# Which engine asks for the down weights: moving one expert weight in three from SyncE's queue to ScalarE's

## The reference, cut to what matters

```python
def hier_moe(xn, w_gr, b_gr, w_er, b_er, w_gate, w_up, w_down):
    ...
    def expert_block(args):
        tok_b, e = args
        xb = xpad[tok_b]
        h = jax.nn.silu(xb @ w_gate[e]) * (xb @ w_up[e])
        return h @ w_down[e]
    ...
    out = out.reshape(rows, d) * buf_wt[:, None].astype(out.dtype)
    y = jnp.zeros((t + 1, d), out.dtype).at[buf_tok].add(out)[:t]
```

## Time and profile before

| | us |
|---|---|
| median of three runs | 1744.66 |
| lowest and highest | 1743.45, 1745.66 |
| the profiled execution | 1749.66 |
| its span | 1747.6 |
| expert stage in it, about | 170 to 677 |
| one pair of experts at full TensorE clock | 30.5 |

### The profile page before, as it was taken

One profiled execution on the slowest core, in us unless ns is written; L12 is line 12 of the kernel. 1 busy time (PEld: TensorE's weight loads), 2 busy tenths in 40 slices (PEclk: granted clock), 3 DMA queues, 4 the chain that ended last, 5 costly groups with the idle time before them and its releaser, 6 DMA issues.

```text
span 1747.6 us, 24578 instructions
## 1 busy us (share of the span) xinstructions
PE 1628.3 (93%) x9324; PEld 1305.9 (75%) x9324; DVE 1249.0 (71%) x1537; ACT 780.7 (45%) x1021; POOL 393.5 (23%) x184
## 2 busy tenths in 40 slices
PE   7995899999999997999988999999999999999997
PEld 7855555555555554988678999999999978888886
DVE  5244888878888886765315996566777788888886
ACT  4413777767777774456033334666666400000000
POOL 6601211111111110000234889422222100000000
PEclk9996899999999998999999999999999999999999
DMA  8407799999999988533312444444444555555553
GB/s 315 154 1 302 304 421 409 415 373 392 421 408 411 413 345 275 193 121 121 145 49 92 175 169 166 150 148 151 141 152 150 187 193 186 194 194 194 192 192 120
DMA packets 45902, 398.87 MB, mean 228 GB/s; under 512 B 10120, under 2 KB 12424, under 8 KB 13576
## 3 DMA queue, kind: packets, MB, share of 16 engines
q1 hardware_dynamic: 45832, 397.89, 59.4%
HBM read 395.77 MB, written 3.01 MB: 228 GB/s over the span
## 4 chain that ended last, share of the span: by engine, by line
PE 38%; POOL 6%; issue 4%; DMA 1%; DVE 1%; ACT 0%; DVEq 0%; POOLq 0%; SPq 0%
PE bank L1834 19%; PE bank L1771 9%; POOL rest L1010 6%; PE bank L1775 5%; PE bank L1805 3%; PE bank L763 1%; DMA raw<-in_v 1%; POOL ring_rest L742 0%; DVE lead L2305 0%; DVE h L2404 0%; ACT half_lead L736 0%; DVE hid_lo L2379 0%; DVE h L2407 0%; DVE xhat L656 0%; DVEq L188 0%
## 5 line engine op out<-in xcount | busy, mean ns | idle before, releaser
L2067 DVE TENSOR_TENSOR ring_rest<-ring,w_lead 128x2048 fp32r<-128x2048 f32 x128 | 293.4, 2343 | 37.7 <-ACT w_lead L1144 37.7
L1144 ACT ACTIVATE w_lead<-ring 128x2048 fp32r<-128x2048 f32 x128 | 239.4, 1905 | 22.1 <-DVE ring_rest L2067 21.7
L647 ACT ACTIVATE xhat<-h 128x1024 f32<-128x1024 f32 x6 | 6.3, 1057 | 432.9 <-DVE h L2404 351.8
L1571 PE MATMUL bank<-ring_rest,x_two 128*128 128x512 f32 x512 | 140.9, 408 | 31.7 <-DVE ring_rest L2067 31.7
L1289 ACT ACTIVATE lead<-raw 128x2048 fp32r<-128x2048 f32 x64 | 122.4, 1913 | 88.7 <-PE bank L1775 88.7
L1834 PE MATMUL bank<-lead,hid_hi 128*128 128x512 f32 x512 | 157.9, 390 | 2.7 <-DVE hid_lo L2379 2.6
L1834 PE MATMUL bank<-lead,hid_lo 128*128 128x512 f32 x512 | 157.7, 389 | 0.0
L1834 PE MATMUL bank<-rest,hid_hi 128*128 128x512 f32 x512 | 157.6, 389 | 0.0
L1571 PE MATMUL bank<-w_lead,x_two 128*128 128x512 f32 x512 | 145.9, 423 | 11.8 <-POOL x_two L993 6.6
L1775 PE MATMUL bank<-nT_hi,rest 128*128 128x256 f32 x1024 | 144.7, 284 | 9.7 <-POOL rest L1010 9.7
L742 POOL TENSOR_TENSOR ring_rest<-ring,half_lead 128x2048 fp32r<-128x2048 f32 x20 | 92.4, 4627 | 264.2 <-ACT half_lead L736 255.0
(11 more groups left out here) (331 smaller groups left out, 2831.0 us busy)
## 6 DMA issues: line engine op xcount, KB each, us to landing
ring<-in_w_gate SPq DMA_DIRECT2D x32, 2048.0 KB, 9.4
ring<-in_w_up SPq DMA_DIRECT2D x32, 2048.0 KB, 9.6
ring<-in_w_down SPq DMA_DIRECT2D x32, 2048.0 KB, 10.4
raw<-in_u SPq DMA_DIRECT2D x64, 1024.0 KB, 4.8
raw<-in_v SPq DMA_DIRECT2D x64, 1024.0 KB, 4.8
ring<-in_w_in SPq DMA_DIRECT2D x14, 2048.0 KB, 10.1
ring<-in_w_out SPq DMA_DIRECT2D x4, 2048.0 KB, 7.8
ring<-in_w_q SPq DMA_DIRECT2D x4, 2048.0 KB, 7.9
```

The lines of the kernel that those rows point to most:

```text
L1144: act.activation(w_lead[half][:, :, :], ring8(slot)[:, 4 * half:4 * half + 4, :], ACT.Copy).then_inc(w_lead_ready, 1)
L1571: last = pe.matmul(bank[kind][:, :], x_two[j][:, 4 * half + k, :], part[:, k, :], start=(ready is w_lead_ready and half == 0 and k == 0), ...
L2067: dve.tensor_tensor(ring_rest8(slot)[:, part, :], ring8(slot)[:, part, :], w_lead[half][:, :, :].bitcast(F32), ALU.subtract).then_inc(w_re ...
```

## The change

The function that gives the address of an expert weight is moved out of SP's block, so that both engines can use it. SP keeps the gate and up loads, now in one plain loop over the pairs, and no longer waits for `down_done` in it. ACT issues the down loads: after both halves of the gate `split_lead` of expert e it waits for `down_done`, issues the load of the down weight of expert e, and then runs `copy_out` of expert e-2 as before. The loads of the first pair all stay on SP. The branch that does not run with these inputs gets the same treatment.

```diff
-            def reload(i, pair):
-                j, kind = PAIR[i]
-                if kind == 2:
-                    sp.wait_ge(down_done, 4 * pair + 2 * j - 2)
-                else:
-                    sp.wait_ge(w_used, 4 * pair + 2 * j + kind - 3)
+                sp.wait_ge(w_used, 4 * pair + 2 * j + kind - 3)
                 sp.dma_start(ring[W_SLOT[i]][:, :], expert_source(i, pair)).then_inc(ring_full[W_SLOT[i]], 16)
-            for i in (0, 1, 3, 4, 2):
-                reload(i, 1)
-            with sp.Fori(2, PAIRS) as pair:
-                reload(0, pair)
-                reload(1, pair)
-                reload(5, pair - 1)
-                reload(3, pair)
-                reload(4, pair)
-                reload(2, pair)
-            reload(5, PAIRS - 1)
+            with sp.Fori(1, PAIRS) as pair:
+                for i in (0, 1, 3, 4):
+                    reload(i, pair)
...
+            def reload_down(j, pair):
+                slot = W_SLOT[3 * j + 2]
+                act.dma_start(ring[slot][:, :], expert_source(3 * j + 2, pair)).then_inc(ring_full[slot], 16)
...
                     split_lead(e, pair, j, 0, first, [1] if first else range(2))
                     if not peeled:
+                        act.wait_ge(down_done, 2 * e - 2)
+                        reload_down(j, pair)
                         copy_out(e - 2, j, bank[3])
```

More of the change, by code:

```diff
@@ L801, in build, with expert_source @@
         W_SLOT = [(CH_MOE + i) % RING for i in range(RING)]
+        def expert_source(i, pair):
+            j, kind = PAIR[i]
+            w = dram[("w_gate", "w_up", "w_down")[kind]]
+            return w[bass.ds(2 * pair + j, 1)].rearrange("e p f -> p (e f)")
         GATHER_BANK = [0, 1, 2, 3, 6, 7, 0, 1]
@@ L861, in _ @@
             sp.dma_start(gain_row[:, :], dram["final_gain"].broadcast_to([P, D])).then_inc(gain_in, 16)
-            def expert_source(i, pair):
-                j, kind = PAIR[i]
-                w = dram[("w_gate", "w_up", "w_down")[kind]]
-                return w[bass.ds(2 * pair + j, 1)].rearrange("e p f -> p (e f)")
             for i in (0, 1, 3, 4, 2, 5):
@@ L1125, in _ @@
                                    bank[4 + half][:, :], ACT.Copy).then_inc(many_weighted, 1)
-                many_scalar(0, True)
-                with act.Fori(1, N_EXPERTS) as e:
-                    many_scalar(e, False)
+                for j in range(2):
+                    many_scalar(j, j == 0)
+                with act.Fori(1, PAIRS) as pair:
+                    for j in range(2):
+                        act.wait_ge(down_done, 4 * pair + 2 * j - 2)
+                        reload_down(j, pair)
+                        many_scalar(2 * pair + j, False)
                 act.wait_ge(many_stored, 16 * N_EXPERTS * BLOCKS_MAX)
```

## The result

| us, median (lowest to highest) | before | changed |
|---|---|---|
| timed runs, 5 each | 1745.57 (1743.45 to 1746.95) | 1774.07 (1767.75 to 1789.73) |
| profiled execution, its span | 1749.66, 1747.6 | 1778.26, 1776.3 |

The changed kernel is slower by 28.5 us in the medians. The ratio, which is formed from all the runs and not from the two medians, is 1.0178, with a 95% interval of 1.0127 to 1.0228. Its runs also spread over 22 us, where those of before spread over 3.5.

What follows compares the result with a forecast made beforehand. The expert stage was taken as bound by a closed ACT, DVE and PE chain, not loads. Issue 8.4 plus clock falls 15.4 gave 23.8 us, so 1768.5 us on the 1744.66 median; range 1748 to 1785.

Steps and rivals of the forecast that it cites:

- What bounds: Expert stage: a closed dependency cycle through ACT, DVE and PE sets 30.5 us a pair; loads run at least 10.4 us ahead.
- the chain: Expert stage: the closed cycle of ACT, DVE and PE steps, without play, that sets the 30.5 us of a pair.
- SP gains nothing: SP's load issues: removing two waits and two issues a pair makes nothing earlier that is waited for; worth nothing.
- The j = 1 half costs nothing: ACT in the j = 1 half: wait and issue are worked off while the second lead is computed; no cost.
- The 0.85 us of play: ACT in the j = 1 half: the next lead waits for DVE from 408.20 to 409.05, enough to cover the issue.
- The other half costs 0.6 us a pair: ACT between the down product and `copy_out`, 14 places: the issue adds 0.6 us each, 8.4 us in all.
- The clock: PE clock in the expert pairs: five more falls than now at 3.08 us each, 15.4 us.
- Seven: Expert pairs: forecast number of the 14 with a clock fall, five more than in the kernel before.
- the term: Expert pairs: the forecast cost of more clock falls, 5 x 3.08 = 15.4 us.
- the 23.8 said: Whole kernel: forecast slowdown, 8.4 us for the issue plus 15.4 us for more clock falls.
- the gap: PE around 408 to 411, waiting for DVE ahead of the gate rests; said to precede clock falls, in every pair.

Runs made afterwards that it cites:

- the issue behind `copy_out`: Changed kernel with ScalarE issuing the down load after `copy_out` instead of before it: 1747.0 us, ratio 1.0015.
- the split in twelve: Kernel before, all loads on SP, with `copy_out` of the j = 0 experts cut into twelve activations instead of two: 1782.26 us, ratio 1.0218.
- the two profiles: Profiled executions of the changed kernel: the original one, and one from running it again unaltered, whose timed runs gave 1775.91 us, ratio 1.0192.
- The filled kernels: Twelve unread matmuls added behind the j = 1 gate lead products: changed kernel 1749.81 us, kernel before 1740.69, changed kernel with issue also behind `copy_out` 1743.37.

## Why the prediction was right, point by point

- **What bounds.** Loads run ahead of their use. In the changed kernel too no engine is seen waiting for one, and with all later down loads on the second queue but off the chain the time is that of before within 0.3% (the issue behind `copy_out`). The page's nine tenths of DMA were no bound.
- **SP gains nothing.** Its emptier queue brought nothing: the kernels with part of the down loads or all of them taken off SP, but off the chain as well, are at the time of before.
- **The j = 1 half costs nothing.** Right, and by the mechanism named: the issue is worked off under the second lead, and the kernel with this half alone is at a ratio of 1.0011. The 0.85 us of play, which I named as the cover, was not needed.
- **The other half costs 0.6 us a pair.** Measured 0.57 in the pair and 0.59 at `copy_out`. The bounds were SP's 0.333 and 0.65; ACT's issue is 0.344, and the rest is the wait and register instructions around it. 8.0 us where 8.4 was said. One detail was off: PE's wait in front of the last up matmuls was to grow to 0.9 us and grew to 0.64. The rest stands at the second half of the up leads, where PE now waits for ACT as well.
- **The clock.** The reason given was that a pair with a fall would last just the distance at which falls recur. The experiments bear it out: at 33.6 us a pair two falls follow one another and then none comes (the kernel before, the issue behind `copy_out`, the j = 1 loads alone), at 34.1 us they go on to the end of the stage, with the DMA (the changed kernel) and without it (the split in twelve), and at 34.8 us they stay single. How many there would be did not follow from this. Seven was the middle between none and fourteen, no more, and that nine and eight came in the two profiles is in part luck. By the first profile the term was too small by 6.1 us, 21.5 against 15.4. That is more than the whole gap between the 28.5 us measured and the 23.8 said; the issue, 0.4 us less than forecast, and the 0.8 us by which the account exceeds the spans go the other way. The cost of one fall was right: 3.08 us was taken, which the earlier trace rows give only as about 3.0 of matmul time, and 3.07 was measured.
- **What stays open.** Two executions of one kernel differ in which pair is the first to fall, so something that the program's own order does not set decides it. None of the runs shows what, nor why falls can recur after 34.1 us.
- **The Trainium skill** ("DMA: Bandwidth & Descriptors", "Rules for kernel authors") says that spreading DMAs over SP and ACT brings no bandwidth and only saves issue time. The runs agree: with the issue behind `copy_out` the loads on two queues move 414 GB/s, as they did on one. The issue time that is saved on SP was idle time anyway, and it is spent on ACT. The Trainium skill ("TensorE: Matmul & The Clock Gate", "What's actually happening") says that activity releases the throttle. The filled kernels agree, with PEclk at 1.00 in their pairs: useless matmuls in the gap took the falls out of the pairs.

## What to carry to other kernels

A DMA issue is cheap on an engine whose stream runs ahead of its arithmetic, and dear directly behind the semaphore that the engine has been idle for: put it one instruction behind the work that the others wait for. Where TensorE waits in a loop near the edge of keeping its clock, a few tenths of a microsecond more in the loop can cost several times their own length (here 0.57 us in each of 14 pairs, 8.0 us in all, cost 28.5), so look at the granted clock pair by pair and not only at the waits. If the gap can't be closed, it can be filled with matmuls that nobody reads, as long as what they make late is not on the chain. Here they ran to 403.06, past the first awaited rest, which was there by 402.45, where ScalarE's lead that waits for it starts, and this cost nothing, because TensorE still had to wait 0.62 us for the next.

## What the runs showed of the hardware

- The time is no monotone function of a delay in the loop: 0.14, 0.32, 0.57 and 1.23 us more in each pair, by the splits of `copy_out` alone, gave medians of 1747.9, 1753.2, 1782.3 and 1768.5 us, and 0, 0, 9 and 3 falls in the pairs of the profiled executions.
- A fall of the granted clock in this stage lasted 6.8 us at 0.50 (1.2 GHz) and cost 3.07 us. It came behind two waits of TensorE, of 0.8 and 1.0 us, with 1.2 us of matmuls between them; the trace shows no longer wait of TensorE in the pairs.
- Small activations that follow one another on ScalarE overlap: each further one lengthened the copy by about 0.057 us (24 in place of two took 1.26 us more), though each by itself lasts some 0.27 us at 128 columns.
- A DMA issue on ScalarE is 0.344 us, against 0.333 on SyncE, and leaves an activation that is being computed undisturbed: the two leads took 3.70 us with an issue under them and without.
